# Start addresses of the two weight tiles and of the streamed tiles, moved to different distances modulo 512 bytes

## The reference

```python
h = rmsnorm(x, mix_norm_w)
proj = h @ w_in                                   # 1024 x 3072
y_ret = retention_group(q, k, v, g, ...)          # 4 heads, chunks of 128, both directions
y_conv = conformer_conv_group(a, b, ...)          # 31 taps, per channel
x = x + concat([y_ret, y_conv]) @ w_out           # 1024 x 1024
x = x + memory_cross_attention(rmsnorm(x), rmsnorm(mem), w_xq, w_xkv, w_xo)
hm = rmsnorm(x, mlp_norm_w)
x = x + square(relu(hm @ w_ff1)) @ w_ff2          # 1024 x 4096, 4096 x 1024
return rmsnorm(x, final_norm_w)
```

## Time and profile before

| | |
|---|---|
| median of 3 runs | 3159.15 us (3158.76 to 3161.02) |
| profiled execution, its own time | 3160.33 us |
| its span | 3158.5 us (1.8 us lie outside) |
| TensorE, matmuls | 2892.5 us busy, 92% of the span |
| TensorE, weight loads | 2372.0 us, 75% |
| VectorE / GpSimd / ScalarE | 1736.6 us (55%) / 1341.8 us (42%) / 519.6 us (16%) |
| granted TensorE clock, mean | 0.958 of full |

### The profile page before, as it was taken

The page is one execution under the profiler, slowest core; times in us unless marked ns, Lnnn a source line. Parts: engine busy times, 40 slices in busy tenths (PEclk is TensorE's granted clock), DMA queues, the critical chain, the costliest instruction groups (busy, mean ns, idle before and its releaser), DMA issues.

```text
span 3158.5 us, 37551 instructions
## 1 busy us (share of the span) xinstructions
PE 2892.5 (92%) x13220; PEld 2372.0 (75%) x13220; DVE 1736.6 (55%) x1734; ACT 519.6 (16%) x910; POOL 1341.8 (42%) x668
## 2 busy tenths in 40 slices
PE   4999999977769889999999999998899999999997
PEld 3888888865548677788888888776777888888886
DVE  8898989896655545641514234655446415142344
ACT  5100000024542222100100001132221001000012
POOL 7475556646633212443435353232124434353531
PEclk6999999989979999999999999999999999999999
DMA  6222222273342111111111113231111111111111
GB/s 217 87 81 89 93 83 88 98 221 115 133 157 63 53 46 33 40 47 53 46 46 46 46 50 102 65 122 53 46 34 40 47 52 48 46 46 47 49 50 60
DMA packets 268084, 232.40 MB, mean 74 GB/s; under 512 B 7888, under 2 KB 229256, under 8 KB 263816
## 3 DMA queue, kind: packets, MB, share of 16 engines
q1 hardware_dynamic: 240688, 167.80, 17.4%
q10 hardware_dynamic: 27352, 64.07, 5.7%
HBM read 179.93 MB, written 51.90 MB: 73 GB/s over the span
## 4 chain that ended last, share of the span: by engine, by line
PE 79%; DVE 10%; issue 5%; POOL 2%; ACT 2%; DMA 1%; DVEq 0%; ACTq 0%; SPq 0%; POOLq 0%
PE ps L589 25%; PE ps L584 24%; PE ps L585 24%; DVE acc L1280 1%; DVE zfin L1591 1%; POOL wlo L444 1%; DVE alo L1418 1%; PE ps L818 1%; PE ps L716 1%; POOL cv L503 1%; PE ps L750 1%; PE ps L819 0%; PE ps L820 0%; DVE st_b L1381 0%; PE ps L808 0%
## 5 line engine op out<-in xcount | busy, mean ns | idle before, releaser
L442 POOL TENSOR_SCALAR whi<-wraw 128x1024 fp32r<-128x1024 f32 x216 | 257.8, 1193 | 1572.0 <-PE ps L589 1269.2
L584 PE MATMUL ps<-ahi,whi 128*128 128x512 f32 x1536 | 603.7, 393 | 32.4 <-DVE alo L1418 20.0
L585 PE MATMUL ps<-alo,whi 128*128 128x512 f32 x1536 | 600.0, 391 | 0.0
L444 POOL TENSOR_TENSOR wlo<-wraw,whi 128x1024 fp32r<-128x1024 f32 x216 | 584.4, 2706 | 18.0
L584 PE MATMUL ps<-bhi,whi 128*128 128x512 f32 x1280 | 502.1, 392 | 0.0
L585 PE MATMUL ps<-blo,whi 128*128 128x512 f32 x1280 | 498.4, 389 | 0.0
L589 PE MATMUL ps<-ahi,wlo 128*128 128x512 f32 x1536 | 381.2, 390 | 0.0
L1577 DVE TENSOR_TENSOR res<-ps,res 128x512 f32 x128 | 88.6, 692 | 519.5 <-PE ps L589 519.5
L584 PEld LDWEIGHTS ps<-ahi,whi 128*128 128x128 f32 x1536 | 289.9, 189 | 102.0 <-DVE alo L1418 18.5
L1280 DVE SCALAR_TENSOR_TENSOR acc<-upad,taps,acc 128x2048 f32<-128x2048 f32 x120 | 349.4, 2912 | 8.8 <-DVE acc L1277 0.6
L585 PEld LDWEIGHTS ps<-alo,whi 128*128 128x128 f32 x1536 | 290.1, 189 | 59.8 <-issue 0.5
(11 more groups left out here) (229 smaller groups left out, 3406.9 us busy)
## 6 DMA issues: line engine op xcount, KB each, us to landing
wraw<-in_w_ff SPq DMA_DIRECT2D x128, 512.0 KB, 3.7
proj_d<-st ACTq DMA_DIRECT2D x64, 256.0 KB, 2.4
wraw<-in_w_in SPq DMA_DIRECT2D x24, 512.0 KB, 3.8
wraw<-in_w_xkv SPq DMA_DIRECT2D x16, 512.0 KB, 3.8
xT_d<-xf SPq DMA_DIRECT2D x32, 256.0 KB, 3.4
wraw<-in_w_out SPq DMA_DIRECT2D x16, 512.0 KB, 3.5
res<-xT_d ACTq DMA_DIRECT2D x16, 512.0 KB, 6.2
wraw<-in_w_xq SPq DMA_DIRECT2D x16, 512.0 KB, 3.4
```

The source lines that it names most:

```text
L442: pool.tensor_scalar(whi[:, slot, :, :], wraw[:, slot, :, :], 1.0, 0.0, ALU.mult, ALU.add).then_inc(w_hi, 1)
L444: pool.tensor_tensor(wlo[:, slot, :, :], wraw[:, slot, :, :], whi[:, slot, :, :], ALU.subtract).then_inc(w_ready, 1)
L584: nc.tensor.matmul(o, whi[:, slot, k, :], hi(k), start=(k == order[0]), stop=False)
L585: nc.tensor.matmul(o, whi[:, slot, k, :], lo(k), start=False, stop=False)
```

## The change

Pads are allocated ahead of tiles, in lines of 64 bytes per partition (16 float32). The pad of 160 bytes moves from before `wraw` to behind it. No instruction is added, removed or moved, and no size, loop, semaphore or transfer changes.

```diff
-        alloc(es, "to_4096", [P, 40], F32)
+        LINE = 16
+
+        def skip(stack, name, lines):
+            alloc(stack, name, [P, lines * LINE], F32)
         wraw = alloc(es, "wraw", [P, 2, KT, P], F32)
+        alloc(es, "to_512", [P, 40], F32)
         whi = alloc(es, "whi", [P, 2, KT, P], F32R)
+        skip(es, "before_wlo", 1)
         wlo = alloc(es, "wlo", [P, 2, KT, P], F32R)
...
         with ExitStack() as s1:
+            skip(s1, "before_xhi", 5)
             xhi = alloc(s1, "xhi", [P, KT, NS, NC], F32R)
+            skip(s1, "before_xlo", 1)
             xlo = alloc(s1, "xlo", [P, KT, NS, NC], F32R)
...
+            skip(s2, "before_q", 6)
...
-            bhi, ahi, alo = (b3(n, (P, KT, NH, NC), F32R) for n in ("bhi", "ahi", "alo"))
+            bhi = b3("bhi", (P, KT, NH, NC), F32R)
+            skip(s3, "before_ahi", 3)
+            ahi = b3("ahi", (P, KT, NH, NC), F32R)
+            skip(s3, "before_alo", 1)
+            alo = b3("alo", (P, KT, NH, NC), F32R)
+            skip(s3, "before_blo", 5)
             with ExitStack() as over:
                 zfin = b3("zfin", (P, KT, NH, NC), F32, over)
             blo = b3("blo", (P, KT, NH, NC), F32R)
```

## The result

The changed kernel takes 3208.24 us (median of 4 runs, 3200.27 to 3210.38) against 3158.95 for the one before (4 runs, 3158.43 to 3161.02): ratio 1.015, 95% interval 1.0132 to 1.0169, 49 us slower. The forecast was no change. In the changed kernel L597, L598 and L602 are what L584, L585 and L589 were; in the kernels of the experiments the same three lines have other numbers again, and the tiles' names tell them apart.

What follows compares the result with a forecast made beforehand. The prediction took the start-to-start distance of TensorE's large matmuls to bound the kernel. Its terms for matmuls, GpSimd, transfers, VectorE and ScalarE summed to 0, so 3159 us as before, range 3075 to 3235.

Steps and rivals of the forecast that it cites:

- What bounds the kernel: TensorE: start-to-start distance of 10,752 large matmuls, 226.7 ns each, 77% of the span; one nanosecond on each is 10.75 us.
- the choice of 0 for the matmuls: TensorE's large matmuls: new distances between streamed and weight tiles leave the 13.4 ns surplus unchanged, so 0 us.
- The bound for a gain: Large matmuls: float32 matmuls against mean_mat show 2.8 ns surplus; 10.6 ns gained on each of 9472, 100 us.
- The bound for a loss: Large matmuls: those that never settle take 231 ns, as after a wait, 4.6 ns more each.
- The lost pace: Rival: large matmuls with alternating distances stay unsettled, 3192 us, or 3209 if L589 does too; chance 0.27.
- The queue behind the load: Rival: TensorE's stream catches up with the weight load and follows at half pace, 178 us more, 3337; chance 0.09.
- The rival of a gain: Rival: new distances free TensorE's stream, -100 us, 3059 in full, 3100 to 3125 in part; chance 0.24.
- Its counterargument: Against the gain: modulo 512 the stream crosses the weight load's place once wherever it starts; a new start only moves the meeting.
- The page on the ports: Skill page giving TensorE two independent read ports and no waiting; by it alone the change is worth nothing.
- The other parts: GpSimd and transfers into wraw cost 0; VectorE and ScalarE taken as 0, with a bound of 3 us either way.
- The range: Whole-kernel time from 3075 to 3235 us, leaving out the fullest gains and the queue, together some 0.17.
- its likeliest case: Whole kernel: no change beyond 0.2% (6.3 us), 3159 us, own range 3153 to 3165; chance 0.40.

Runs made afterwards that it cites:

- e1: Kernel before with four 64-byte lines ahead of whi, moving whi, wlo and every tile behind together: 3161.06 us, ratio 1.000.
- e2: Kernel before with whi and wlo at 0 and every streamed tile at 4 lines: 3159.51 us, ratio 1.0004.
- e5: Kernel before with whi, wlo at 0, xhi, xlo at 1 line, bhi, blo at 2, ahi, alo at 3: 3211.41 us, ratio 1.0167.
- e6: Kernel before with whi, wlo at 0, xhi, xlo at 5 lines, bhi, blo at 6, ahi, alo at 7: 3210.76 us, ratio 1.0165.
- e9: Kernel before with whi, wlo at 0, xhi, xlo at 3 lines, bhi, blo at 1, ahi, alo at 2: 3202.71 us, ratio 1.014.
- e13: Kernel before with whi, wlo at 0, xhi, xlo at 6 lines, bhi, blo at 1, ahi, alo at 4: 3176.61 us, ratio 1.0049.
- e3: Kernel before with only the low streamed tiles (xlo, alo, blo) one line later: 3205.56 us, ratio 1.0148.
- e4: Kernel before with wlo alone one line later, whi and streamed tiles at 0: 3188.9 us, ratio 1.0091.
- e7: Kernel before with only the 160-byte pad moved behind wraw, so wraw starts at 5.5 lines: 3159.0 us, ratio 0.9999.
- e8: Kernel before with eight lines (512 bytes) ahead of each of xhi, ahi and blo: 3160.51 us, ratio 1.0001.
- e10: Kernel before with whi, wlo at 0, xhi, xlo at 0.5 line, bhi, blo at 2.5, ahi, alo at 3.5: 3226.48 us, ratio 1.0205.
- e12: Kernel before with pads in four-line steps, so each product alternates between distances 0 and 4 lines: 3160.71 us, ratio 1.0001.
- e14: Kernel before with mhi and mlo 3 lines later and kh 7, wide matmuls left at 0: 3159.96 us, ratio 0.9998.

## Why the prediction was wrong

**What bounds the kernel** was right: the distance between the starts of the large matmuls sets the time, and one nanosecond on each is worth 10.75 us. The 4.6 to 5.4 ns seen give 55 us, of which 49 arrived.

**The step that failed** is the choice of 0 for the matmuls: "What costs the same whatever is being read looks like the exchange of the weights rather than a clash of addresses." All the rows that it rests on, a, b and x tiles, 512 columns and 256, have distance 0. They agreed because nothing in them varied what was in question. The term put at 0 measured some 5 ns on each large matmul. The settled values, 24 matmuls at a time, are: 5.44 us at 0 and 4 lines, 5.49 to 5.50 at 1 and 5, 5.57 to 5.61 at 2 and 6, 5.60 at 3 and 7, 5.60 to 5.62 at half lines (e1, e2, e5, e6, e9 to e13). So 2 to 7.5 ns of a surplus of up to 21 depend on the distance, and changing it at every matmul costs about 5 even between two cheap ones (e3). What the 13.4 ns at distance 0 consist of stays open: no run took them away.

**The bound for a gain** (2.8 ns against `mean_mat`) was a row of another form, which takes two cycles a column, as the prediction said, and it didn't carry over: at two lines the fp32r pairs have 19 ns over 213.3, not 2.8. Whether the rate is the reason was not tried.

**The bound for a loss** was right to 1 ns. Unsettled matmuls were taken at 231 ns; the changed kernel runs at 231 to 232, and e4 shows the settling behind each change of distance. Some of that is luck: L602 with `ahi` runs at 233 to 234 because that is the settled value of three lines, and not because it is unsettled.

**The rivals.** The lost pace gave 3192 to 3209 us, and 3208 was measured. Its mechanism is part of it: it had only the changes of distance, and e13 shows that one distance inside each product still costs 17 us. It also expected one distance to settle at 227 ns, which e5 refutes. That it had the time right owes something to both effects lying near 232 ns. The queue behind the load is out by e2. The rival of a gain expected some distances below 226.7; of the seven other distances tried modulo 256 bytes, whole and half lines, none is. Its counterargument, that stream and load cross once whatever the start, wasn't tested.

**The page on the ports.** "SBUF — State Buffer" in the Trainium skill (section "Who interferes with whom") has TensorE's two read ports independent and TensorE waiting on nobody. Taken as a time, it says that e5 and e1 are alike; they differ by 50 us. The measurement decides: where the one read starts relative to the other changes TensorE's pace.

**The other parts** were right. `wraw` half a line off costs nothing (e7), GpSimd kept its cover, and VectorE's sum rose by 3.5 us over the execution.

**The range** held the time, and its likeliest case, given 0.40, was not the one.

## What to carry to other kernels

A surplus that is the same in every row is no sign of a constant of the machine if the layout is the same in every row; ask what the rows have in common before calling it fixed. For streams of 512 fp32r columns with a weight load for each, start weight tiles and streamed tiles at the same place modulo 256 bytes, all of them, high and low; a pad of 64 bytes ahead of one kind of tile cost 0.9% (e4) to 1.5% (e3) of this kernel, which is bound by its matmuls. Change one distance at a time: several at once measured neither the distance nor the change of it.

## What the runs showed of the hardware

- The distance between two starts of 128x512 fp32r matmuls at the full clock depends on the distance between the start of the streamed tile and that of the weights, modulo 256 bytes: 226.7 ns at 0, about 229 at 64, 232 to 233 at 128, 233 at 192, 233 to 234 at 32, 96, 160 and 224 (e1, e2, e5, e6, e8 to e13). The starts themselves don't matter as long as both move together: by 256 bytes (e1), or by 128 and 160 in the outputs of the attention (e5, e10).
- The pace has a memory. After a wait, or after a change of that distance, it takes several matmuls, at 232 ns in the mean, to come back to 226.7: five or six behind a change (e4), two to ten behind a wait (the kernel before). Where the distance changes at every matmul by 64 bytes it doesn't (e3); where it changes by 256 bytes there is nothing to come back from (e12).
- Matmuls of 256 columns take 120.0 ns at distance 0 and no more than that at any other: 118.0 for the scores at 192 bytes (e14). Their distance doesn't fix their pace: at 192 bytes the products with `mhi` and `mlo` take 117.8 ns in e14 and 115.6 in e9.
- Which part of the chip the two reads share was not tried.
